# Three-pass input projections, a half swap on VectorE and a convolution in later slots, in a hybrid decoder step

## The reference

```
u = adaLN_modulate(x, c)
one combined projection of u -> heads of A, B, C, D and the gates g0..g3
A: mLSTM matrix memory (aq, ak, av, ao)    B: latent attention (kv, bq, paged cache)
C: GLU(ca, cg) -> causal depthwise conv, width 31 -> layer norm -> silu
D: retention: rotary(dq), rotary(dk), dv, gate dg, state S per head
rotary(x) = [x1*cos - x2*sin, x1*sin + x2*cos]       x1, x2 the halves of a head
sum over n of sigmoid(g_n) * (branch_n @ W_n)  -> output projection -> DeepNorm
SwiGLU FFN -> DeepNorm
```

## Time and profile before

| what | value |
|---|---|
| median of 3 runs | 2072.83 us (2067.87 to 2073.23) |
| profiled execution, its own time | 2086.45 us |
| its span, first to last instruction | 2084.6 us |
| mean granted TensorE clock | 0.944 of full |
| DMA, mean over the span | 148 GB/s, 308.97 MB |
| ACT, DVE, POOL busy | 30%, 40%, 24% |
| chain that ended last | PE 38%, DVE 4%, DMA 2% |

### The profile page before, as it was taken

How to read it: one execution, slowest core, us unless ns; L and a number is a source line. 1 busy time by engine, 2 the same in 40 slices (tenths; PEclk the granted TensorE clock), 3 DMA queues, 4 the chain that set the end, 5 groups by cost and what they waited for, 6 DMA issues and landing times. The chain is left out here.

```text
span 2084.6 us, 28429 instructions
## 1 busy us (share of the span) xinstructions
PE 1936.5 (93%) x10290; PEld 1504.4 (72%) x10290; DVE 831.0 (40%) x1841; ACT 620.7 (30%) x1028; POOL 493.7 (24%) x342
## 2 busy tenths in 40 slices
PE   4999999999999989999869999999999999899997
PEld 2676776687556779999736767667865567699996
DVE  1242489363211364333313334893622123633333
ACT  1224202131333334443303242021422332344422
POOL 0000273033012123333100001820420122233331
PEclk9999989998999999999959999899989999899999
DMA  8242254225675244444064334342266652544431
GB/s 332 100 157 98 64 121 142 99 88 201 208 259 202 106 171 168 147 147 153 37 249 162 109 90 75 109 156 96 71 222 221 223 203 106 201 143 157 147 141 46
DMA packets 81168, 308.97 MB, mean 148 GB/s; under 512 B 23746, under 2 KB 33282, under 8 KB 50946
## 3 DMA queue, kind: packets, MB, share of 16 engines
q1 hardware_dynamic: 81026, 307.12, 42.8%
HBM read 291.85 MB, written 15.25 MB: 147 GB/s over the span
## 5 line engine op out<-in xcount | busy, mean ns | idle before, releaser
L435 PE MATMUL zps<-u,ring 128*128 128x320 f32 x1728 | 493.1, 446 | 5.4 <-DVE u L1356 5.4
L435 PEld LDWEIGHTS zps<-u,ring 128*128 128x128 f32 x1728 | 337.6, 197 | 149.6 <-issue 20.9
L1930 POOL TENSOR_TENSOR wlo<-ring,whi 128x1024 fp32r<-128x1024 f32 x66 | 161.1, 2440 | 368.0 <-ACT whi L1013 368.0
L874 PE MATMUL zps<-xhi,whi 128*128 128x320 f32 x704 | 220.1, 313 | 1.5 <-DVE xlo L1815 1.5
L875 PE MATMUL zps<-xlo,whi 128*128 128x320 f32 x704 | 219.3, 311 | 0.0
L876 PE MATMUL zps<-xhi,wlo 128*128 128x320 f32 x704 | 219.2, 311 | 0.0
L1013 ACT ACTIVATE whi<-ring 128x1024 fp32r<-128x1024 f32 x132 | 140.1, 1061 | 102.0 <-PE zps L876 93.9
L1916 POOL TENSOR_TENSOR wlx<-ring,whg 128x1024 fp32r<-128x1024 f32 x32 | 77.8, 2432 | 325.9 <-ACT whg L1013 323.2
L420 PE MATMUL zps<-y,ring 128*128 128x320 f32 x512 | 140.6, 433 | 1.0 <-issue 1.0
L874 PEld LDWEIGHTS zps<-xhi,whi 128*128 128x128 f32 x704 | 133.8, 190 | 2.5 <-DVE xlo L1815 2.2
L875 PEld LDWEIGHTS zps<-xlo,whi 128*128 128x128 f32 x704 | 133.8, 190 | 0.0
(11 more groups left out here) (262 smaller groups left out, 2953.4 us busy)
## 6 DMA issues: line engine op xcount, KB each, us to landing
ring<-wpack_dram SPq DMA_DIRECT2D x222, 1024.0 KB, 4.9
arena<-cache_dram SPq DMA_DIRECT2D x128, 320.0 KB, 3.4
arena<-stateA_dram SPq DMA_DIRECT2D x2, 2064.0 KB, 10.4
o_cn_s<-arena SPq DMA_DIRECT2D x2, 2064.0 KB, 6.3
arena<-stateD_dram SPq DMA_DIRECT2D x2, 2048.0 KB, 11.8
o_ret_s<-arena SPq DMA_DIRECT2D x2, 2048.0 KB, 9.1
x<-o_y SPq DMA_DIRECT2D x2, 1280.0 KB, 7.4
o_y<-x SPq DMA_DIRECT2D x4, 640.0 KB, 3.0
```

The lines of the kernel that those rows point to most:

```text
L435: last = nc.tensor.matmul(ps[:, 0:T], w[:, (j * KC + k) * P:(j * KC + k + 1) * P], uk[k], start=k == 0, stop=k == KC - 1)
L874: nc.tensor.matmul(o, hi[:, cols], xh, start=start, stop=False)
L1930: G().tensor_tensor(wlo[q % 2][:, 1024:2048], ring[:, (FIRST_FFN + q) % RING, 1024:2048], whi[q % 2][:, 1024:2048], ALU.subtract).then_inc ...
```

## The change

All "in" blocks go through `split_tile`, with one rounded buffer of two halves, `wh`, for every block. ACT rounds half a block when the block before has released it (`after`), POOL makes all rests, its other work is put between them (one or more conv pairs behind each), and the rest of u is made on DVE inside the modulation (`u_low`); the first tile waits for it piece by piece. `swapD` and its products are gone: DVE reads the two halves of the tile in PSUM crosswise and adds the bias itself, and its third piece frees the bank. The products of queries with states are 32-wide pieces in two column places. Gate 3 and its branch (of D) come before gate 2 (of the convolution), so the sample slots hold gate 2. The taps are spread as the list `TAPS` says, and the convolution's sums and norm move into slot 1.

```
-GATE_ORDER = (0, 2, 3, 1)
+GATE_ORDER = (0, 3, 2, 1)
-SLOTS = [[("gate", 3, 0)],
-         [("ada", 8), ("gate", 3, 2), ("ada", 9)],
+SLOTS = [[("gate", 2, 0)],
+         [("ada", 8), ("gate", 2, 2), ("ada", 9)],
...
+TAPS = (0, 8, 16, 24, 40, 52, 60, 84, 100, 124)
+SPLIT = [b for b in BLOCKS if b[0] in ("in", "out")]
...
+                            split_tile(q, n, j, name, free[j], uhi, ulo, "dve_ul" if first and j == 0 else None)
...
-                                    mms = [(w_[0:NS, 384:448], vtok[0:NS, 2, h, 0:width])]
-                                    mms += [(qz[:, b * 256 + h * NS:b * 256 + (h + 1) * NS], state[:, b, h, 0:width]) for b in range(NB)]
+                                    nc.tensor.matmul(o, w_[0:NS, 384:448], vtok[0:NS, 2, h, 0:width], start=True, stop=False)
+                                    for r in range(4):
+                                        for g in range(2):
+                                            at0 = 512 * g + 128 * r + 32 * h
+                                            last = nc.tensor.matmul(ps[32 * g:32 * g + 32, i * width:(i + 1) * width], qz[:, at0:at0 + 32],
+                                                                    state[:, 4 * g + r, h, 0:width], start=False, stop=r == 3)
...
-                            s = "act_dz" if x_ in ("dk", "dq") else "act_d"
-                            in_tiles((f"{x_}{j}", f"{x_}{j + 1}"), [(s, (x_, j)), (s, (x_, j + 1))])
+                            free = [("dve_dk", ("t3", x_, h)) if x_ in ("dk", "dq") else ("act_d", (x_, h)) for h in (j, j + 1)]
+                            in_tiles((f"{x_}{j}", f"{x_}{j + 1}"), free)
...
-                            if s == "act_dz":
-                                swap(x_, j)
-                                swap(x_, j + 1)
...
                     outputs("d", 0, P)
                     scores("d", 2)
                     scores("d", 3)
+                    gate(3, 0)
                     outputs("d", 1, P)
                     state_prompt("d", P)
-                    gated(2, 0)
                     state_sample("d", 0, P)
-                    gate(2, 4)
+                    gate(3, 2)
                     for b in range(1, NB):
                         state_sample("d", b, P)
                     for t in range(3):
                         turn_heads("d", t)
-                    gate(2, 6)
-                    branch(2, 4)
+                    branch(3, 0)
+                    gated(3, 4)
...
+                            if q >= 1:
+                                act.wait_ge(*at("pe_h", (q - 1, i)))
+                                act.wait_ge(*at("pool_l", (q - 1, i)))
+                            go("act_hq", (q, i), wh[:, i, :], ring[:, n % RING, i * 1024:(i + 1) * 1024], ACT.Copy)
...
+                    gates(3, 0, 2)
                     prompt_state("d", P)
+                    gates(3, 2, 2)
                     for t in range(3):
                         head_std("d", t)
-                    gates(2, 4)
+                    gates(3, 4)
...
-                        V().tensor_tensor(dst, tmp[:, h % 2, :], cs("cosD"), ALU.mult).then_inc(*ev("dve_dk", ("t1", x_, h)))
-                        V().tensor_tensor(std[:], m(("sw", x_, h))[:, 0:T], cs("sinD"), ALU.mult).then_inc(*ev("dve_dk", ("t2", x_, h)))
+                        V().scalar_tensor_tensor(out=dst, in0=ps[:, 0:T], scalar=bias, in1=cs("cosD"), op0=ALU.add, op1=ALU.mult).then_inc(*ev("dve_dk", ("t1", x_, h)))
+                        for i, (to, of) in enumerate((((0, 64), (64, 128)), ((64, 128), (0, 64)))):
+                            V().scalar_tensor_tensor(out=std[to[0]:to[1], :], in0=ps[of[0]:of[1], 0:T], scalar=bias[of[0]:of[1]], in1=cs("sinD")[of[0]:of[1]],
+                                                   op0=ALU.add, op1=ALU.mult).then_inc(*ev("dve_dk", (f"t{2 + i}", x_, h)))
...
-                        taps(12 * i, 12 * (i + 1) if i < 3 else 4 * CW)
+                        taps(TAPS[i], TAPS[i + 1])
...
+                    taps(TAPS[5], TAPS[6])
                     head_rows("d", 1, P)
-                    gated(2, 0)
                     head_norm("d")
+                    taps(TAPS[6], TAPS[7])
                     state_update("d", P)
+                    taps(TAPS[7], TAPS[8])
                     head_gate("d", 3)
-                    gated(2, 4)
+                    gated(3, 0)
+                    taps(TAPS[8], TAPS[9])
+                    gated(3, 4)
...
+                    for i, name in enumerate(("dq0", "dq2", "dv0", "dv2", "dg0", "dg2")):
+                        low_of(name)
+                        conv_taps(i, i + 1)
...
                     batch_keys("d", 2, NB)
+                    for i, name in enumerate(("g3_4", "g3_6")):
+                        low_of(name)
+                        conv_taps(14 + 8 * i, 22 + 9 * i)
```

More of the change, by code:

```diff
@@ L85 @@
 NBLK = len(BLOCKS)
-SPLIT = [b for b in BLOCKS if b[0] == "out" or b[0] == "in" and b[1] in [f"g{n}_{i}" for n in GATE_ORDER[1:] for i in range(8)]]
+SPLIT = [b for b in BLOCKS if b[0] in ("in", "out")]
 RING = 3
+ARENA = 16512
 TILES = (["small", "kv0", "kv1", "bq0", "bq1", "bq2"] + [f"{x}{i}" for x in ("aq", "ak", "av", "ao", "ca", "cg", "dq", "dk", "dv", "dg") for i in range(4)]
@@ L421, in group @@
                         last.then_inc(*ev("pe_" + kind, name))
[L423 to L438, removed]
                     def split_tile(q, n, j, name, freed_by, xh, xl, ready=None):
-                        o, hi = bank("z", name, freed_by)[:, 0:T], high_buffer(q)[j]
+                        o, hi = bank("z", name, freed_by)[:, 0:T], wh[:, j, :]
                         pe.wait_ge(*at("act_hq", (q, j)))
@@ L453, in split_tile, with in_tiles @@
                         last.then_inc(*ev("pe_z", name))
+                    def in_tiles(names, free, first=False, between=None):
+                        q = SPLIT.index(("in",) + names)
+                        n, _ = weights(("in",) + names)
+                        for j, name in enumerate(names):
+                            if between and j == 1:
+                                between()
+                            split_tile(q, n, j, name, free[j], uhi, ulo, "dve_ul" if first and j == 0 else None)
+                        block_end[n] = ("pe_z", names[-1])
                     def ada(a0, a1, through=True):
@@ L1167, in _, with gates @@
                     gate_seq = [(n, d) for n in GATE_ORDER[:3] for d in range(8)]
-                    def gates(n, half, count=4):
+                    def gates(n, half, count=4, follow=True):
                         for i in range(half, half + count):
-                            block = ("in", f"g{n}_{i - i % 2}", f"g{n}_{i - i % 2 + 1}")
-                            if block in SPLIT:
-                                q = SPLIT.index(block) + 1
-                                if BLOCKS[BLOCKS.index(block) + 1][0] != "ada" and SPLIT[q][0] == "in" and SPLIT[q][1] != "g3_0" and (q, i % 2) != (1, 0):
-                                    high(q, (i % 2,))
+                            if follow and (n, i) != (1, 7) and (n, i) != (1, 6):
+                                after(f"g{n}_{i}", i % 2)
                             if n == GATE_ORDER[3]:
@@ L1679, in _ @@
                     weigh("d", 1)
-                    ps = m("conv sum")
-                    for j in range(4):
-                        V().scalar_tensor_tensor(out=y[:, 2, j, :], in0=ps[:, 0:T], scalar=-1.0 / CCH, in1=y[:, 2, j, :], op0=ALU.mult,
-                                               op1=ALU.add).then_inc(*ev("dve_c", ("mu", j)))
+                    taps(TAPS[4], TAPS[5])
                     gated(0, 4)
@@ L1845, in G, with low, low_of @@
                         return nc.gpsimd
+                    def low(q):
+                        n = BLOCKS.index(SPLIT[q])
+                        for i in range(2):
+                            pool.wait_ge(*at("act_hq", (q, i)))
+                            half = slice(i * 1024, (i + 1) * 1024)
+                            G().tensor_tensor(wlx[:, n % RING, half], ring[:, n % RING, half], wh[:, i, :], ALU.subtract).then_inc(*ev("pool_l", (q, i)))
+                    def low_of(name):
+                        low([q for q, b in enumerate(SPLIT) if name in b[1:]][0])
                     G().memset(r4[:], 0.0).then_inc(*ev("pool_z", "r4"))
+                    G().memset(qz, 0.0).then_inc(*ev("pool_z", "qz"))
+                    G().memset(vtok[:, :, :, P:W], 1.0).then_inc(*ev("pool_z", "ones"))
+                    for name in ("small", "kv1", "bq1", "ao0"):
+                        low_of(name)
                     pool.wait_ge(*at("dve_b", "kpe"))
```

242 lines of the change are left out of this document (128 added, 114 removed).

## The result

The changed kernel takes 2147.68 us (median of 4 runs, 2140.31 to 2151.64), the kernel before 2073.03 beside it: a ratio of 1.0361, 95% interval 1.0323 to 1.0398. It is 3.6% slower. The prediction said 2078, with 2030 to 2112 as its range: the time lies 36 us above it, and 5 us above the 2143 that the forecast got with every one of its bounds at the bad end.

The account below looks back on a forecast made before the run. PE (TensorE), busy 93% of the span, was taken as the bound. Losses of 65.4 us against gains of 62.7 gave +2.7 a layer, +5 in all; 2086.45 + 5 - 13.6 = 2078 us, range 2030 to 2112.

Parts of the forecast that it names:

- bounds at the bad end: Case with every term at its worst bound: +35 us a layer, 2143 us.
- Start: First tiles behind DVE's chain for u, lengthened by eight subtractions: 9 us lost a layer, bounds 3 and 14.
- Three passes: "In" blocks on PE: a tile every 3.52 us, 7.04 instead of 8.62 a block, 42.7 us gained over 27 blocks.
- Outputs: Head outputs' state-query products as 32-column pieces: 1.7 of 4.0 us gained a call, 6.8 in four; bounds nothing and 3.0 a call.
- A blocks and mLSTM: Prompt attention's softmax steps must fit beside 7.04 us blocks and share ports with POOL's rests: 1 us lost, bounds 0 and 7.
- Rotations: dk and dq blocks: DVE's rotations and taps take 12.0 us against PE's 7.04; 17.9 us lost a layer, bounds 5 and 26.
- rival 3: dk and dq stage: rests hold DVE their whole length, taps average over 1.1 us; 8 us more a layer, 2094; chance 0.18.
- State of d: State products and branch(3,0): PE stalls 15.7 and 13.6 us behind DVE; 32 us lost a layer, bounds 25 and 36.
- Slot 1 and the gates before it: ACT work ahead of gate(2,2)'s costs 2.9 us, 24 taps behind gated(3,0) leave DVE 2.6 behind: 5.5 lost, bounds 0 and 8.
- SP's loads: Block loads of 1 MB: they have room where PE goes faster, as PE never waits for `ring` after the start.
- The basis: Starting time: the profiled execution of 2086.45 us, with 13.6 taken off for its excess over the median of 2072.83.

Follow-up runs that it names:

- e5: e4 with no taps between the rotations of dk0 to dq0, those 24 placed in twos behind tiles dv0 to g0_3: 2054.60 us, ratio 0.9895.
- e2: Changed kernel with the 24 taps behind head_norm(d) moved in front of it: 2124.30 us, ratio 1.0261.
- e3: Changed kernel with head_gate(d) directly behind state_update and the 16 taps between them joined to the 24 behind gated(3,0): 2117.05 us, ratio 1.0216.
- e1: Changed kernel with ACT's rounding of block g2_0 moved from ahead of the sigmoids of g3_6 and g3_7 to sample slot 0: 2119.07 us, ratio 1.0225.
- e10: The kernel of e5 run again unchanged, on another chip: one time, 2046.12 us.
- e9: e4 with two taps moved from the row behind gated(3,0) to the row before head_norm, so 38 stay: one time, 2083.28 us.
- e4: Changed kernel with the edits of e1, e2 and e3 together: 2084.99 us, ratio 1.0071.
- e8: The kernel of e4 run again unchanged: one time, 2081.93 us.

## Why the prediction was wrong

**Start: right in size.** The first tile started at 53.72 and u's chain was slower, as put; when PE reaches the A blocks the difference is +2.0 us, where 6.3 of gain (four blocks) less 9 gives +2.7.

**Three passes: right.** Tiles follow at 3.52 us wherever nothing holds them, and PE's busy time fell by 84 us. I had put 112. Longer records at the slow clock are part of the other 28: the 512 branch records, which the change leaves alone, took 152.0 us (458 ns each) where they took 140.6 (433). The rest was not traced record by record.

**Outputs: right.** The sample products of a pair of heads are two groups like this one (PE's timeline of the changed kernel):

```profile
221.34 1.07 PE L606 MATMUL mps<-arena 128*32 128x129 f32 x16
```

That is 2.1 us where 4.0 were spent, 1.87 times as fast, and 1.8 us gained a call where I took 1.7. The Trainium skill's factor of up to 4 for 32 columns (TensorEngine Tiling (Array Packing), Theoretical Speedup) would have needed 1.0 us; two column places that alternate gave about two.

**A blocks and mLSTM: 4 us too good.** Waits of 2.73 and 3.44 us on DVE (1.44 stood in the place of the second before) and 0.96 on ACT appear in a stretch for which I had put 1 (bounds 0 and 7).

**Rotations: right in sum, by luck in part.** I put 14.9 us of stalls behind three blocks plus 3 for the clock. The nine blocks from dk2 to g0_2 took 82.9 us, 19.5 over nine times 7.04: two stalls and two short waits, 12.3 in all, and 7.2 of longer records. Fewer stalls and a dearer clock cancelled. e5 shows the cause, the taps between the rotations; in this profile rests held them, as rival 3 had it, but in two of the three rows only, and the 22 taps of the three rows took 0.86 on the mean, near my 0.82 and under the 1.1 of that rival. What I had left out is the wait in state_sample(a), 4.29 us for DVE's state update: PE comes to it earlier by 14.6 us and DVE does not. And spreading the queries was not costed at all, though the change doubles it from four to eight instructions beside POOL: 3.5 us more, most of the 4.7 by which the stage before g0_4 was missed.

**State of d: right.** Predicted stalls of 15.7 and 13.6, measured 16.50 and 15.04; e2 took the taps' share out of the first, e3 the second.

**Slot 1 and the gates before it: here the prediction failed.** Its step was "24 taps at 0.82 between gated(3,0) and gated(3,4) last 19.7 us ... 2.6 behind", and "SP's loads: ... they have room, as PE never waits for `ring`". The taps took 9.59 us, 0.40 each, and it was POOL that stood: its two rests took 11.85 us beside them, and PE waited 3.56 at the third pass. And the load of g2_0 was asked for by ACT, not by PE, with two sigmoids queued behind it: 10.80 us, e1. I had looked for what PE waits for on each queue and not for what an engine that PE waits for has in front of it. Of the 16.1 us by which the stage up to the first sample scores was missed, these two waits are 11.8 (14.4 where I had 2.6) and the two state stalls 2.2. PE's busy time there fell by 2.2 us where my terms make 5.0; the branch block of 477.83 alone took 2.6 us longer than the 8.77 of e1's at the full clock. Slot 1 itself lost 3.08 where I had put 2.9.

**The basis.** I compared with a profiled execution 13.6 us over its median and took that off; the profiled execution of the changed kernel lay 3.3 under its own. The 17 us of this stay unexplained.

In all 27.5 us a layer were missed: 4.1, 5.2, 4.7 and 16.1 less 2.5. The two waits on POOL and ACT are the largest part, but not all of it: had they cost the 2.6 us I gave them, the forecast would still have been some 31 us too low instead of 55 between the profiled executions, and the median near 2124, still above the range.

## What to carry to other kernels

A rounding, a copy or a DMA wait that is put ahead of an instruction which frees a buffer is on the critical path even if its own result is not needed for another 17 us (the rounding of g2_0 began at 519.85, PE used it at 537.41): walk the queue of each engine that PE waits for, and ask what each wait in it has ahead. Filler work goes where the trace shows the engine idle before a wait, not after it: the same 24 taps cost 10 us a layer behind head_norm and nothing before it. With VectorE and GpSimd both on SBUF, keep rows of VectorE work shorter than the slack of GpSimd's next result (rows of 24 and 40 taps cost PE 3.56 and 9.89 us there, a row of 8 nothing).

## What the runs showed of the hardware

Contention between DVE and POOL on SBUF has two outcomes. A rest of 2.43 us that meets a row of taps either ends in 2.6 us and holds one tap for that long, or it stands until the row is over: 15.65 us with 40 taps, 14.86 with 38, 9.32 with 24. The Trainium skill (SBUF — State Buffer, "SBUF: two separate sides") says that the side which starts first "gets the pair for the whole instruction". The trace agrees as far as one instruction goes, but in the second case the next taps got the port again and again, 0.40 us each, with the rest already waiting. The same program did either in different executions (e5 and e10) and in the two layers of one (e9), the rest starting 2.47 us into the row each time, 0.1 us behind the start of a tap. The row won in both layers of the changed kernel and of e1 to e4, e8 and e10, the rest in both of e5. What tips it, no run here shows.
